# Three norm borders whose first two feed-forward products are taken before the norm's root

## The reference

```
h = x * rsqrt(mean(x*x) + eps) * norm_g * (1 + scale) + shift      # scale, shift, gate: columns from c @ ada_w
x = x + 0.5 * gate * ((silu(h @ Wa) * (h @ Wb)) @ w_down)          # four feed-forward sublayers: F0, F1, F2, F3
```

## Time and profile before

| | |
|---|---|
| median of 3 runs | 2416.41 us (2414.57 to 2418.41) |
| profiled execution, its own time | 2417.73 us |
| span in the profile, first to last instruction | 2416.1 us |
| mean granted TensorE clock | 0.994 of full speed |
| PE busy | 2379.4 us, 98% |
| DVE busy | 1273.5 us, 53% |
| ACT busy | 861.5 us, 36% |
| weights and other data read from HBM | 281.85 MB, 119 GB/s over the span |

### The profile page before, as it was taken

The page is one execution under the profiler, slowest core; times in us unless marked ns, Lnnn a source line. Parts: engine busy times, 40 slices in busy tenths (PEclk is TensorE's granted clock), DMA queues, the critical chain, the costliest instruction groups (busy, mean ns, idle before and its releaser), DMA issues.

```text
span 2416.1 us, 30379 instructions
## 1 busy us (share of the span) xinstructions
PE 2379.4 (98%) x11030; PEld 1905.1 (79%) x11030; DVE 1273.5 (53%) x1951; ACT 861.5 (36%) x1320; POOL 202.4 (8%) x337
## 2 busy tenths in 40 slices
PE   7999999999999999999999999999999999999998
PEld 4888888677788888888888888888888888867766
DVE  6886334455678873343333355555533333459654
ACT  4222223566542232242322243344422222344453
POOL 1212000000001210000000013331000000120200
PEclk9999999999999999999999999999999999999999
DMA  8899432322259973223333321212233333232211
GB/s 274 272 287 292 118 95 65 100 60 60 64 167 288 287 231 111 86 75 99 95 99 108 89 79 53 62 53 79 84 99 95 95 110 95 68 97 62 62 53 53
DMA packets 420385, 285.27 MB, mean 118 GB/s; under 512 B 22690, under 2 KB 397788, under 8 KB 420304
## 3 DMA queue, kind: packets, MB, share of 16 engines
q1 hardware_dynamic: 397888, 207.64, 29.7%
q0 software_dynamic: 20896, 73.80, 9.3%
q10 hardware_dynamic: 1520, 2.77, 0.4%
HBM read 281.85 MB, written 6.72 MB: 119 GB/s over the span
## 4 chain that ended last, share of the span: by engine, by line
PE 92%; DVE 3%; ACT 2%; DMA 1%; SPq 1%; issue 1%; POOL 0%; ACTq 0%; DVEq 0%; POOLq 0%
PE bank L682 13%; PE bank L684 13%; PE bank L683 13%; PE bank L850 7%; PE bank L852 7%; PE bank L851 7%; PE bank L1493 4%; PE bank L1495 4%; PE bank L1494 4%; PE bank L1520 2%; PE bank L717 2%; PE bank L719 2%; PE bank L718 2%; PE bank L1142 1%; PE bank L1115 1%; PE bank L697 1%
## 5 line engine op out<-in xcount | busy, mean ns | idle before, releaser
L638 DVE TENSOR_TENSOR w_lo<-raw,w_hi 128x1024 fp32r<-128x1024 f32 (+1 forms) x331 | 434.1, 1312 | 425.6 <-ACT w_hi L619 421.0
L619 ACT ACTIVATE w_hi<-raw 128x1024 fp32r<-128x1024 f32 (+1 forms) x331 | 369.8, 1117 | 481.6 <-PE bank L684 242.7
L682 PE MATMUL bank<-h_hi,w_hi 128*128 128x512 f32 x1344 | 523.1, 389 | 1.1 <-DVE w_lo L638 1.1
L683 PE MATMUL bank<-h_lo,w_hi 128*128 128x512 f32 x1344 | 522.9, 389 | 0.0
L684 PE MATMUL bank<-h_hi,w_lo 128*128 128x512 f32 x1344 | 522.8, 389 | 0.0
L682 PEld LDWEIGHTS bank<-h_hi,w_hi 128*128 128x128 f32 x1344 | 252.2, 188 | 53.9 <-DVE w_lo L638 2.0
L683 PEld LDWEIGHTS bank<-h_lo,w_hi 128*128 128x128 f32 x1344 | 252.3, 188 | 52.6
L684 PEld LDWEIGHTS bank<-h_hi,w_lo 128*128 128x128 f32 x1344 | 252.3, 188 | 52.6
L850 PE MATMUL bank<-g_hi,w_hi 128*128 128x512 f32 x704 | 277.8, 395 | 0.0
L852 PE MATMUL bank<-g_hi,w_lo 128*128 128x512 f32 x704 | 276.0, 392 | 0.0
L851 PE MATMUL bank<-g_lo,w_hi 128*128 128x512 f32 x704 | 273.2, 388 | 0.0
(11 more groups left out here) (417 smaller groups left out, 3052.1 us busy)
## 6 DMA issues: line engine op xcount, KB each, us to landing
raw<-in_ffn_w_in SPq DMA_DIRECT2D x176, 512.0 KB, 3.9
ada<-in_ada_w POOLq DMA_DIRECT2D x128, 512.0 KB, 5.0
raw<-in_ffn_w_down SPq DMA_DIRECT2D x64, 704.0 KB, 4.6
raw<-in_hgrn_w_in SPq DMA_DIRECT2D x32, 512.0 KB, 4.1
raw<-in_attn_w_qkv SPq DMA_DIRECT2D x24, 512.0 KB, 3.8
raw<-in_w_in SPq DMA_DIRECT2D x22, 512.0 KB, 3.8
ada_first<-in_ada_w SPq DMA_DIRECT2D x16, 512.0 KB, 10.8
bias_scratch<-bias_lines POOLq DMA_DIRECT2D x14, 320.0 KB, 9.0
```

Of the source, the lines that this page charges most:

```text
L619: line(nc.scalar.activation(w_place(n, 0, k * P)[0], raw[:, n % 4, 0:k * P], ACT.Copy), hi_ready)
L638: line(nc.vector.tensor_tensor(lo, raw[:, n % 4, 0:k * P], hi.bitcast(F32), ALU.subtract), lo_ready)
L682: nc.tensor.matmul(out_ap, wh, xh, start=(k == 0), stop=False)
L683: nc.tensor.matmul(out_ap, wh, xl, start=False, stop=False)
```

## The change

It concerns the borders m = 2, 3 and 5 (`DEFERRED`). As the tiles of x become final, ACT and DVE make u = x * scale_col, without the root, split into `h_hi` and `h_lo`. The first two blocks of the next stage are multiplied with u (`deferred_pair`), and the bank is multiplied by `rstd` afterwards. The shift is brought in as one number for each output feature: DVE sums the weight tiles times the shift columns (`shift_sum_dve`, 8 instructions on 128x128 for each of the two blocks), PE adds them up over the partitions, and the number is added at silu and at the gate product. The other blocks use h as before; it is written over u tile by tile (`deferred_norm_act`, `deferred_norm_dve`). The `idle_turns` of these borders go. The third block's product waits for `h_ready` tile by tile; in the first turn of `up` ACT and DVE split only block n + 4, and the silu of bank 0 waits for `unscaled` and takes `shift_col` as its bias. `lower(j)` is the instruction that writes `h_lo` tile j, as in `norm_dve`.

```diff
+        DEFERRED = (2, 3, 5)
+        U_AT = {2: {3: (0, 1), 4: (2, 3), 5: (4, 5), 6: (6,), 7: (7,)}}
+        def u_tiles(m, j):
+            return U_AT[m].get(j, ()) if m in U_AT else (j,)
+        def u_hi_act(act, line, m, j, i=None):
+            for k in u_tiles(m, j):
+                xj, hi, _, scale = u_parts(k, i)
+                line(nc.scalar.activation(hi, xj, ACT.Copy, scale=scale), uhi_ready)
+        def u_lo_dve(dve, line, m, j, i=None):
+            for k in u_tiles(m, j):
+                dve.wait_ge(uhi_ready, plus(i, 2, KD * deferred_before(m) + k + 1))
+                xj, hi, lo, scale = u_parts(k, i)
+                line(nc.vector.scalar_tensor_tensor(out=lo, in0=xj, scalar=scale, in1=hi.bitcast(F32), op0=ALU.mult,
+                                                    op1=ALU.subtract), ulo_ready)
+        def shift_sum_dve(dve, line, m, b):
+            n = FIRST[NEXT[m]] + b
+            acc = tmp[:, 3, b * P:(b + 1) * P]
+            dve.wait_ge(landed[n % 4], landings(n))
+            for k in range(KD):
+                tile = raw[:, n % 4, k * P:(k + 1) * P]
+                s = mod[:, 24 * m + k:24 * m + k + 1]
+                line.settle()
+                if k == 0:
+                    line(nc.vector.tensor_scalar(acc, tile, s, None, ALU.mult))
+                else:
+                    line(nc.vector.scalar_tensor_tensor(out=acc, in0=tile, scalar=s, in1=acc, op0=ALU.mult, op1=ALU.add),
+                         shift_sum if k == KD - 1 else None)
+        def deferred_pair(pe, m, banks):
+            pe.wait_ge(shift_sum, 2 * (d + 1))
+            for b in range(2):
+                last = nc.tensor.matmul(B[4][:, b:b + 1], tmp[:, 3, b * P:(b + 1) * P], ones[:, 0:1], start=True, stop=True)
+            last.then_inc(shift_ps, 1)
+            for b in range(2):
+                pe.wait_ge(x_ready, KD * m + KD - 1 + b)
+                pe.wait_ge(lo_ready, n + b + 1)
+                for k, (uh, ul) in enumerate(H_TILES):
+                    if b == 0:
+                        pe.wait_ge(ulo_ready, KD * d + k + 1)
...
+                    if b == 0 and k == 2:
+                        pe.wait_ge(sum_full, d + 1)
+                        nc.tensor.matmul(B[5][:, :], ones[:, :], sumsq[:, :], start=True, stop=True).then_inc(rms_ps, 1)
+        def deferred_norm_act(act, line, m, after):
+            norm_root_act(act, line, m)
+            if after:
+                nc.scalar.preload_act_table(after)
+            first_half_hi(act, line, m)
+            split_hi(act, line, n + 2)
+            for j in range(KD):
+                if j < KD - 1:
+                    act.wait_ge(u_used, (KD - 1) * d + j + 1)
+                else:
+                    act.wait_ge(used, n + 2)
+                act.wait_ge(t_ready, KD * m + j + 1)
+                line(nc.scalar.activation(h_hi[:, j, :], tmp[:, j % 4, :], ACT.Identity,
+                                          bias=mod[:, 24 * m + j:24 * m + j + 1]), hhi_ready)
+            split_hi(act, line, n + 3)
+        def deferred_norm_dve(dve, line, m):
...
+            for j in range(KD):
+                if j >= 4:
+                    dve.wait_ge(h_ready, KD * m + j - 3)
+                line(nc.vector.scalar_tensor_tensor(out=tmp[:, j % 4, :], in0=xT[:, j, :],
+                                                    scalar=scale_col[:, j:j + 1], in1=rstd[:, :],
+                                                    op0=ALU.mult, op1=ALU.mult), t_ready)
+                if j:
+                    lower(j - 1)
+                if j == 2:
+                    first_half_lo(dve, line, m)
+                    split_lo(dve, line, n + 2)
+            lower(KD - 1)
+            split_lo(dve, line, n + 3)
+            for b in range(2):
+                dve.wait_ge(used, n + b + 1)
+                line(nc.vector.tensor_tensor(B[b][:, :], B[b][:, :], rstd[:, :], ALU.mult), unscaled)
@@ residual_dve
+            if m in DEFERRED:
+                dve.wait_ge(sq_ready, line.value(x_ready))
+                line(nc.vector.tensor_tensor(sumsq[:, :], sumsq[:, :], sq[:, :], ALU.add),
+                     sum_full if j == KD - 1 else sum_ready)
+                u_lo_dve(dve, line, m, j, i)
+                if j == KD - 1:
+                    split_lo(dve, line, n + 2)
+                    line.settle()
+                return
@@ residual_act
+            if stage_after(n) in DEFERRED:
+                u_hi_act(act, line, stage_after(n), j, i)
@@ ffn_dve, down
+                    if m and s and RES_OF[name] in DEFERRED:
+                        for b in range(2):
+                            shift_sum_dve(dve, line, RES_OF[name], b)
                     split_lo(dve, line, n + 2 * s + 2, i)
@@ back_dve
+            if m in DEFERRED:
+                scale_dve(line, m)
             for j in range(KD):
+                if m in DEFERRED and j in (KD - 3, KD - 2):
+                    shift_sum_dve(dve, line, m, j - KD + 3)
@@ tensor program
-            norm_pe(pe, 2)
             ffn_pe(pe, "F1", 1, 9, 9)
-            norm_pe(pe, 3)
             ffn_pe(pe, "F2", 2, 0, 0)
...
-            norm_pe(pe, 5)
             ffn_pe(pe, "F3", 3, 0, 0)
```

More of the change, by code:

```diff
@@ new lines, in deferred_pair @@
+        def deferred_pair(pe, m, banks):
+            n, d = FIRST[NEXT[m]], deferred_before(m)
+            pe.wait_ge(shift_sum, 2 * (d + 1))
+            for b in range(2):
+                last = nc.tensor.matmul(B[4][:, b:b + 1], tmp[:, 3, b * P:(b + 1) * P], ones[:, 0:1], start=True,
+                                        stop=True)
+            last.then_inc(shift_ps, 1)
+            for b in range(2):
+                s = (n + b) % 2
+                pe.wait_ge(x_ready, KD * m + KD - 1 + b)
[3 more added lines that the diff above has]
+                        pe.wait_ge(ulo_ready, KD * d + k + 1)
+                    wh, wl = w_hi[:, s, k * P:(k + 1) * P], w_lo[:, s, k * P:(k + 1) * P]
+                    nc.tensor.matmul(banks[b][:, :], wh, uh, start=(k == 0), stop=False)
+                    nc.tensor.matmul(banks[b][:, :], wl, uh, start=False, stop=False)
+                    last = nc.tensor.matmul(banks[b][:, :], wh, ul, start=False, stop=(k == KD - 1))
+                    if k == KD - 1:
+                        last.then_inc(used, 1)
+                    elif b == 1:
+                        last.then_inc(u_used, 1)
+                    elif k == KD // 2 - 1:
+                        last.then_inc(half_used, 1)
+                    if b == 0 and k == 2:
+                        pe.wait_ge(sum_full, d + 1)
+                        nc.tensor.matmul(B[5][:, :], ones[:, :], sumsq[:, :], start=True, stop=True).then_inc(rms_ps, 1)
@@ new lines, in deferred_norm_dve, with lower @@
+        def deferred_norm_dve(dve, line, m):
+            n, d = FIRST[NEXT[m]], deferred_before(m)
+            line(nc.vector.tensor_scalar(gate_col[:, :], mod[:, 24 * m + 16:24 * m + 24],
+                                         1.0 if m % 3 == 1 else 0.5, None, ALU.mult))
+            dve.wait_ge(shift_ps, d + 1)
+            line(nc.vector.tensor_copy(shift_col[:, :], B[4][:, 0:2]), shift_col_ready)
+            dve.wait_ge(rstd_ready, m + 1)
+            def lower(j):
+                dve.wait_ge(hhi_ready, KD * m + j + 1)
+                line(nc.vector.scalar_tensor_tensor(out=h_lo[:, j, :], in0=tmp[:, j % 4, :],
+                                                    scalar=mod[:, 24 * m + j:24 * m + j + 1],
+                                                    in1=h_hi[:, j, :].bitcast(F32), op0=ALU.add,
+                                                    op1=ALU.subtract), h_ready)
+            for j in range(KD):
[14 more added lines that the diff above has]
+                line(nc.vector.tensor_tensor(B[b][:, :], B[b][:, :], rstd[:, :], ALU.mult), unscaled)
@@ L769, in norm_act @@
         def norm_act(act, line, m, after):
+            if m in DEFERRED:
+                deferred_norm_act(act, line, m, after)
+                return
             if m:
@@ L826, in up @@
                     if m == s == 0:
-                        product_pair(pe, NORM_OF[name], B)
+                        if NORM_OF[name] in DEFERRED:
+                            deferred_pair(pe, NORM_OF[name], B)
+                        else:
+                            product_pair(pe, NORM_OF[name], B)
                         continue
                     for b in range(2):
-                        product(pe, n + 2 * s + b, B[2 * s + b][:, :], H_TILES, i)
+                        fresh = (h_ready, KD * NORM_OF[name] + 1) if b == m == 0 and NORM_OF[name] in DEFERRED else None
+                        product(pe, n + 2 * s + b, B[2 * s + b][:, :], H_TILES, i, waits=fresh)
             up(n0, None, 0)
@@ L998, in up @@
             def up(n, i, m, ada_end, ada_begin):
+                late = NORM_OF[name] in DEFERRED and m == 0
                 for s in range(2):
-                    if m or s:
```

(12 more changed lines are left out.)

62 lines of the change are left out of this document (56 added, 6 removed).

## The result

The changed kernel takes 2433.26 us in the median of four runs (2431.15 to 2436.56), the kernel before 2416.73 in the same measurement: 16.5 us slower, ratio 1.0073 with a 95% interval of 1.0061 to 1.0086. The forecast was 2421.9, slower by 5.5, with a range up to 2428. The direction is right, the size is not: 11 us are missing from the sum. The profiled execution is the longest of the four, 3.3 us above their median.

What follows compares the result with a forecast made beforehand. PE, busy 98% and carrying 92% of the chain of waits, was taken as the bound. Borders -1.6, HO +1.5 and WO +4.4 gave +4.3, plus 1.2 of clock: +5.5 on 2416.4, so 2421.9 us, range 2414 to 2428.

Steps and rivals of the forecast that it cites:

- small terms: scale_dve's column instructions, the clearing of sumsq and moved loads, all borders: fall in waits or have room, together zero.
- The border's value, 1.6 us: Each of three borders: last down matmul to end of fourth product takes 26.6 us against 28.1, worth 1.6 us.
- Shift sums of 2.97 us a block: DVE's chain of small dependent instructions, 0.38 apart: 2.97 us a block, 5.9 for the two blocks of a border.
- Hidden in F1's down side: At border F1 to F2 the 5.9 us of shift sums cost PE nothing, with 2.8 us left.
- The stalls in HO, 1.75 and 1.35: PE waits 1.75 and 1.35 us for DVE's splits around HO's products 5 and 6; HO ends 3.1 later.
- In WO, 3.9 and 2.0: PE waits 3.9 and 2.0 us for splits behind u tiles and shift sums in WO, which ends 5.95 later.
- The clock, 1.2 us at the borders: Slow tiles reaching the fourth product after PE's pieces of standing still: 0.4 us a border, 1.2 for three.
- What comes after has room: After the fourth product's wait, unscaling, silu and the fifth block's split end near 24.4 us, at no cost.
- The rival of free waits between small instructions: Waits between DVE's small instructions cost nothing, pace 0.27: +0.8 and 1.2 of clock, 2418.4 us; chance 0.15.
- The faster rival: Shift sums fit into DVE's idle time in WO and HO; three borders give 4.7 us, 2411.7; chance 0.10.
- The clock everywhere: Clock falls at each border into the fourth product and once more in HO or WO: +9.9, 2426.3; chance 0.13.

Runs made afterwards that it cites:

- experiment 3: The kernel before with an unused tensor of 8 bytes a partition allocated where the change puts shift_col, no instruction added: 2429.45 us, ratio 1.0047 to the kernel before.
- experiment 5: The changed kernel with shift_col as two unused columns of the tensor small, all addresses as in the kernel before: 2423.31 us, ratio 1.0027 to the kernel before.
- experiment 9: The change at border F1 to F2 alone, shift_col inside small, other borders as in the kernel before: 2415.97 us against 2417.16, ratio 0.9995.
- experiment 10: experiment 5 with DVE making tmp tiles 0 to 3 in front of h_lo tile 0: 2420.24 us, ratio 1.0010 to the kernel before.
- Experiments 4: The changed kernel with shift_col of 64 bytes and six of eight weight tiles left out of WO's and HO's shift sums, timing only: 2425.31 us.
- experiment 11: experiment 10 with WO's and HO's shift sums spread over DVE's waits and WO's u tiles made at tiles 4 to 7: 2411.79 us, ratio 0.9974.

## Why the prediction was wrong, step by step

- **The step that failed** is in the small terms, "Zero": the new tensor. The change allocates `shift_col`, and no term of the sum has a price for that. It moved g, y1 and yh by 32 bytes, and 2506 matmuls on them went from 0.229 to 0.233 us apart: 11.0 us by the paces, 12.4 by experiment 3 and 10.0 by experiment 5 (their intervals are 3 to 4 us wide to each side). With it the forecast's own sum gives 2421.9 + 11.0 = 2432.9 where 2433.3 was measured.
- **That 2432.9 lies so near has some luck in it**, for the parts are off in both directions. Lengths in PE's timeline in us; the up sides run from the last matmul of the stage before, border included, to the first on g:

| stretch | forecast of the change | before | experiment 5 | changed kernel |
|---|---|---|---|---|
| WO, first to last matmul on y1 | +5.95 | 57.79 | 64.21 | 64.89 |
| HO, first to last on yh | +3.1 | 43.73 | 47.21 | 47.83 |
| border and up side of F1 | -1.6 | 246.11 | 245.73 | 245.26 |
| of F2 | -1.6 | 245.83 | 244.43 | 244.36 |
| of F3 | -1.6 | 245.83 | 244.43 | 244.42 |
| F1's down side | 0 | 120.85 | 120.85 | 123.18 |

- In experiment 5, with the old place, the first five rows add up to +6.7, where the forecast had 4.3 and 1.2 for the clock; the times say +6.0. In the changed kernel each of the four down sides is 2.3 longer.
- **The border's value, 1.6 us**: nearly right at F1-F2 and HO-F3, too high at WO-F1. 21.0 us to the fourth product against 21.1, in the changed kernel and in experiment 9, and 1.4 us by the rows of F2 and F3; but F1's row gives back only 0.4 in experiment 5 and 0.9 in the changed kernel. That DVE's order is the bound was shown by experiment 10.
- **Shift sums of 2.97 us a block**: right, 0.39 apart. Hidden in F1's down side, as worked out: no PE wait in front of the pair at that border.
- **The stalls in HO, 1.75 and 1.35**: measured 1.64 and 1.13. **In WO, 3.9 and 2.0**: measured 3.69, then none, because product 6 ran 2.5 us longer at the lower clock (1.4 forecast) and took up the second wait; WO so grew by 6.4 in experiment 5 and not by 5.95. Experiments 4 and 11 took the stalls away in two ways and gave 7.5 and 8.4 us.
- **The clock, 1.2 us at the borders**: mis-sized. It fell in WO only; behind 1.64 and 1.13 us in HO and behind the pieces in the third products it held. The forecast said that the wait of 1.75 in HO would bring it down as the one of 3.9 would; it did not. What the sum had too little of lies elsewhere: in experiment 5 0.7 are a wait for a split in F1 behind DVE's ada sums, a step that was put at zero ("What comes after has room"), and 0.5 and 0.4 are in WO and HO. The rest of F1's row is not traced to a cause. The interval of the +6.0 (4.1 to 8.7) holds the 6.7.
- **The rival of free waits between small instructions** is refuted by the 0.39, against the 0.27 that it was estimated at. The rule of the Trainium skill (VectorE: DVE Perf Modes, The DRAIN you can't avoid), that a semaphore after each instruction costs nothing, gave no good price for this chain, in which each instruction needs the one before; no run here has the same chain without the waits. **The faster rival** fell as DVE had no 2.97 us free between a residual and a split; experiment 11 shows that spread out the sums do fit into DVE's idle time. **The clock everywhere** didn't come.
- Small slips of the sum, none of which decides: the border from its own numbers is 28.1 - 26.6 = 1.5, from 2.51, where PE asks for the addition, to 2.56, where it ends, are 0.05 and not 0.15, the rival of free waits adds up to +0.7, three borders of 1.6 are 4.8.

## What to carry to other kernels

Price a new tensor like an instruction: look what is allocated behind it and whether a hot engine reads it, and compare the pace of the same matmul in a stretch without waits, in which nothing but the address can have changed. Where an engine has idle time by the share but is asked in a fixed order, new work costs its full length in front of the instruction that the bound engine waits for, and less in the holes behind it: here WO and HO were 9.6 us longer with the small instructions as blocks in front of a split than with them spread over waits that were there, of which the borders took back 3.2. When a long wait is filled to keep the clock, look also at a schedule that breaks it up: here pieces of 0.3 to 0.5 us left the clock at full without the filling, and a wait of 3.14 at each of three borders did not.

## What the runs showed of the hardware that was not expected

- TensorE's pace in matmuls of 512 fp32r columns (the type of the split parts) changed where the address of the moving tile was all that had changed in what it reads. By the start within 256 bytes: 0.2267 us at 128, 0.2289 at 192, 0.2333 at 224 and at 0. Five places were tried, two of them 256 bytes apart and alike; that the pattern repeats every 256 bytes elsewhere is not shown. Between the best and the worst of them lie 2.9%. Why is open; the Trainium skill (Advanced Engine Details and Errata, SBUF Cachelines) speaks of lines of 16 bytes, but moves by 32 and 64 bytes, which keep that alignment, changed the pace, so such lines alone don't explain it.
- A round address is not by itself a good one: four of the five places are multiples of 64 bytes, with paces of 0.2267, 0.2289 (two) and 0.2333, and the one multiple of 256 was among the two slowest.
- Behind a wait of 1.64 us in the last stage of the kernel before the clock fell to the 1.2 GHz level, some 1.2 us after PE had taken up again, and behind one of the same length in HO of the changed kernel it stayed at full (granted 1.00 from 1734.6 to 1740). PE was busy throughout the 4 us before either wait, so why they differ is open. Behind 3.14 and 3.69 us it fell each time.
